# Modulation chunks of a mixer stage dealt over the second part of its steps only

## What is computed

```
mods = (silu(c) @ ada_w + ada_b).reshape(B, 3, 3, 1, D_MODEL)
def modulate(t, i):
    return t * (1.0 + mods[:, i, 1]) + mods[:, i, 0]
def residual(t, i, out, w):
    return _layer_norm(ALPHA * t + w * (1.0 + mods[:, i, 2]) * out, ln_g[i], ln_b[i])
x = residual(x, 0, _swiglu(modulate(x, 0), ...), 0.5)
o_rw, o_gla, o_ml = rwkv7(proj), gla(proj), mlstm(proj)      # proj = modulate(x, 1) @ w_in
x = residual(x, 1, concatenate([o_rw, o_gla, o_ml]) @ w_out, 1.0)
x = residual(x, 2, _swiglu(modulate(x, 2), ...), 0.5)
```

## Time and profile before

| What | us |
|---|---|
| Median of the runs | 1889.33 |
| The profiled execution | 1889.8 |
| Its span in the trace | 1888.0 |
| TensorE busy with matmuls | 1742.9 |
| VectorE busy | 977.2 |
| ScalarE busy | 678.6 |

### The profile page before, as it was taken

One profiled execution on the slowest core, in us unless ns is written; L12 is line 12 of the kernel. 1 busy time (PEld: TensorE's weight loads), 2 busy tenths in 40 slices (PEclk: granted clock), 3 DMA queues, 4 the chain that ended last, 5 costly groups with the idle time before them and its releaser, 6 DMA issues.

```text
span 1888.0 us, 33548 instructions
## 1 busy us (share of the span) xinstructions
PE 1742.9 (92%) x14420; PEld 1568.9 (83%) x14420; DVE 977.2 (52%) x1623; ACT 678.6 (36%) x949; POOL 170.6 (9%) x217
## 2 busy tenths in 40 slices
PE   5999998988899788999989999989989996899997
PEld 2899997987768477999979999979867765799997
DVE  2444445585633476555454444458574336655544
ACT  2333334463211435333353333355532123543333
POOL 1000011002001021000110000110020011300011
PEclk9999998999855598999999999999988557899998
DMA  8556545423232145444456555463323112344442
GB/s 325 182 199 212 190 150 188 162 95 118 92 118 68 48 151 189 146 149 153 147 176 211 180 184 174 153 209 108 115 70 129 57 48 79 117 157 146 156 145 73
DMA packets 85203, 272.36 MB, mean 144 GB/s; under 512 B 18976, under 2 KB 21312, under 8 KB 84800
## 3 DMA queue, kind: packets, MB, share of 16 engines
q1 hardware_dynamic: 80640, 267.60, 41.7%
q10 hardware_dynamic: 4416, 2.62, 0.5%
HBM read 263.92 MB, written 6.26 MB: 143 GB/s over the span
## 4 chain that ended last, share of the span: by engine, by line
PE 78%; DVE 11%; DMA 4%; ACT 4%; issue 2%; SPq 0%; POOL 0%; DVEq 0%; ACTq 0%; POOLq 0%
PE psV L1824 11%; PE psV L1826 11%; PE psV L1825 11%; PE psA L1824 9%; PE psA L1825 9%; PE psA L1826 9%; DMA raw<-weights_dram 4%; PE psC L1839 3%; DVE wlo L2098 3%; PE psV L671 2%; ACT whi L1980 1%; PE psY L1839 1%; DVE PJ L1357 1%; PE psV L1849 1%; PE psV L1442 1%
## 5 line engine op out<-in xcount | busy, mean ns | idle before, releaser
L2098 DVE TENSOR_TENSOR wlo<-raw,whi 128x1024 fp32r<-128x1024 f32 x344 | 425.1, 1239 | 459.7 <-ACT whi L1980 457.9
L1980 ACT ACTIVATE whi<-raw 128x1024 fp32r<-128x1024 f32 x344 | 362.2, 1055 | 343.8 <-PE psV L1826 338.7
L1824 PE MATMUL psA<-XH,whi 128*128 128x320 f32 x1200 | 381.6, 318 | 20.3 <-DVE XL L2150 11.5
L1825 PE MATMUL psA<-XL,whi 128*128 128x320 f32 x1200 | 375.9, 313 | 0.0
L1826 PE MATMUL psA<-XH,wlo 128*128 128x320 f32 x1200 | 375.5, 313 | 0.0
L1824 PE MATMUL psV<-XH,whi 128*128 128x320 f32 x848 | 269.9, 318 | 13.2 <-DVE wlo L2098 7.2
L1825 PE MATMUL psV<-XL,whi 128*128 128x320 f32 x848 | 266.0, 314 | 0.0
L1826 PE MATMUL psV<-XH,wlo 128*128 128x320 f32 x848 | 265.7, 313 | 0.0
L1824 PEld LDWEIGHTS psA<-XH,whi 128*128 128x128 f32 x1200 | 230.4, 192 | 35.1 <-issue 27.9
L1825 PEld LDWEIGHTS psA<-XL,whi 128*128 128x128 f32 x1200 | 230.2, 192 | 0.3
L1826 PEld LDWEIGHTS psA<-XH,wlo 128*128 128x128 f32 x1200 | 230.0, 192 | 0.0
(11 more groups left out here) (368 smaller groups left out, 1914.1 us busy)
## 6 DMA issues: line engine op xcount, KB each, us to landing
raw<-weights_dram SPq DMA_DIRECT2D x488, 512.0 KB, 3.3
ZS<-st_rw_dram SPq DMA_DIRECT2D x2, 768.0 KB, 4.7
S<-st_gla_dram ACTq DMA_DIRECT2D x2, 768.0 KB, 5.1
o_glas_dram<-S SPq DMA_DIRECT2D x2, 768.0 KB
o_rws_dram<-ZS SPq DMA_DIRECT2D x2, 768.0 KB
CON<-consts_dram SPq DMA_DIRECT2D x1, 1288.5 KB, 9.5
XT<-xT_dram SPq DMA_DIRECT2D x1, 1280.0 KB, 9.8
yT_dram<-XT SPq DMA_DIRECT2D x8, 160.0 KB
```

The costliest lines, as they stand in the source:

```text
L1824: mm(out, whi[:, n % SPL, k], hi[:, kt], start=first, stop=False)
L1825: mm(out, whi[:, n % SPL, k], lo[:, kt], start=False, stop=False)
L1980: activation(whi[:, n % SPL], raw[:, DENSE[n] % RAW], ACT.Copy).then_inc(hi_done, 1)
L2098: tt(wlo[:, n % SPL], raw[:, DENSE[n] % RAW], whi[:, n % SPL].bitcast(F32), ALU.subtract).then_inc(lo_done, 1)
```

## The change

The items of `in_tail` are no longer spread over all 57 steps. `together` is put out bare, and all 40 (or 30) items are spread over the 31 later steps. Nothing else differs: the same chunks in the same order, so `LOADS` is the same list too, and the same mixer steps in the same order.

```
     together = spread([(rw[0], int(k > 1)) for k in range(RW_INVERSE)], first)
     heads, ends = GL_STEPS - GL_FIRST, ML_STEPS - ML_FIRST
     other = (ml + gl) * 6 + su + (ml + gl) * (heads - 6) + su + ml * (ends - heads)
-    together += spread([(rw[0], 1)] * (RW_CHUNKS + RW_SAMPLES - 1), other)
-    out += spread([(step, 1) for step in together], ada_groups(in_tail) if in_tail else [])
+    late = spread([(rw[0], 1)] * (RW_CHUNKS + RW_SAMPLES - 1), other)
+    out += together + spread([(step, 1) for step in late], ada_groups(in_tail))
```

## The result

| What | before | changed |
|---|---|---|
| Median, us (4 runs each, same chip) | 1881.57 (1871.8 to 1890.78) | 1909.4 (1906.18 to 1911.61) |
| Ratio with 95% interval | | 1.0132 [1.0079, 1.0184] |
| Span of the profiled execution, us | 1888.0 | 1906.2 |

The four in the table are two of each group, so that their median, 1881.57, lies where hardly a run is. Eight runs of the changed kernel, e8's among them, lie between 1906.2 and 1921.4, with a median of 1911.2. Set against the large sample the change costs 19 us, 1.0%, and the two traces differ by 18.2 us; the one of before is from the larger group. I go by the traces from here. Each is one execution.

The account below looks back on a forecast made before the run. It took TensorE at the half clock to bound the later steps. Gains of 8.1 and 3.7 against costs of 15.8, 10.3 and 1.0 gave +15.3; with -4.6 from the clock, 1889.8 became 1900.5 us, range 1880 to 1918.

Parts of the forecast that it names:

- the second rival: Steps up to the inverse: without chunks as fillers TensorE idles longer and its clock falls earlier, 1916.5 us; chance 0.23.
- both clock cases: TensorE's clock rising in the later steps (1870 us) or falling in the steps up to the inverse (1916.5 us).
- A1, gain 8.1: First layer, steps up to the inverse: 6.1 us of TensorE's work comes back, and 1.9 us from ScalarE.
- The part that wasn't a matmul: First layer, up to the inverse: without ScalarE's group copy, `gl`'s exponentials start earlier and VectorE's wait goes, gain 1.9 us.
- B1, cost 15.8 + 1.0: First layer, later steps: 13 more chunks and 3 more folds cost 15.8 us, new waits for copies 1.0 us.
- The two new waits: First layer, later steps: at two places a group's first chunk must wait for ScalarE's copy, some 0.5 us each.
- These two I let cancel: Second layer's lost full clock from 1432 to 1446, 5.7 us, set against as much gained in the first layer.
- the 10.3 of the sum: Second layer, later steps: added chunks 10.1 us and folds 0.9 and about 0.3, less 1.0 falling into a wait.
- A2, gain 3.7: Second layer, steps up to the inverse: six chunks and half a microsecond ahead of L718 come back, 3.7 us together.
- L767 in the second layer, -4.6: Near the end of the second layer's steps the clock rises as in the first, shortening L767 and L772, twice 2.3 us.
- The clock rising in B: Later steps: added chunks lift TensorE's clock; 1870 us if a third of the work runs at full clock; chance 0.15.
- The cost hidden: Later steps: slack that the busy figure hides takes up the moved chunks, time about 1890 us; chance 0.05.

Follow-up runs that it names:

- e8: The changed kernel run once more, nothing altered, beside other follow-up runs and the kernel before: 1913.88 us, ratio 1.0118.
- e4: The changed kernel plus 24 idle matmuls, results never read, ahead of L700 in each layer: 1895.14 us, ratio 1.0006.
- e1: The kernel before with the change made in the first layer only: 1901.17 us, ratio 1.0066.
- e9: The changed kernel with only 64 of 256 columns computed in each chunk's matmuls in the mixer steps: 1890.37 us, ratio 1.0008.
- e6: The kernel before, order unchanged, plus 24 idle matmuls ahead of L700 in each layer: 1879.64 us, ratio 0.9916.
- e7: Against the kernel before, all items over the 26 steps up to the inverse, plus 24 idle matmuls ahead of L700: 1877.74 us, ratio 0.9932.
- e2: The kernel before with the change made in the second layer only: 1906.57 us, ratio 1.0076.
- e5: The changed kernel with six of each chunk's eight matmuls left out in the mixer steps: 1911.78 us, ratio 1.0103.
- e10: Against the kernel before, items over the steps up to the inverse and the first eight later ones, plus 24 idle matmuls: 1880.7 us, ratio 0.9974.
- e3: Against the kernel before, the move turned round: all items over the 26 steps up to the inverse, later steps bare: 1879.95 us, ratio 0.9938.
- e11: Against the kernel before: first layer same order plus idle matmuls ahead of L700, second layer all items up to the inverse: 1871.09 us, ratio 0.9933.

## Why the prediction came out as it did

The result, 1909.4 us, lies inside the range of 1880 to 1918 and between the forecast (1900.5) and the second rival (1916.5). The range was made to hold most of both clock cases, so that lying in it says little for the mechanism; by the prediction's own line (up to 1908.2 can't be told from no change, chance 0.60) the time is "slower", to which it gave 0.29. The traces differ by 18.2 us where the sum had 10.7. They say why: the sums over the first layer's instructions held, the second layer's clock didn't, and A2 gave back 0.9 us less than its list of chunks.

**A1, gain 8.1: held, 8.2** (6.7 up to L700, where the list had 6.2, and 1.5 from there to L718, where it had 1.9). There is no instruction on `psC` in A any more. Windows with only instructions on `psC`, A1 and B1, against the earlier trace rows:

```profile
444.40:514.20 69.80, 0.00 (x0) 0.00 (x0) 0.00 (x0) 0.82 0.01 2
514.20:635.60 121.40, 28.43 (x224) 6.10 (x224) 2.28 (x6) 0.53 0.38 125
```

The part that wasn't a matmul came too. The timeline of the changed kernel has `gl`'s exponentials at 493.6 us (the prediction had 498) and VectorE's copy behind them, against the earlier trace rows:

```profile
493.57 0.74 ACT L1206 ACTIVATE GZ<-GB 128x640 f32<-128x640 f32 x1
...
504.66 0.17 DVE L1255 COPY GPC<-GZ 128x8 f32<-128x8 f32 x1
```

VectorE's row has no bracket now, the wait of 1.91 us is gone. (The prediction's "some 9 and 7 us of TensorE's work taken out" doesn't agree with its own bounds, 12.7 and 8.6; no term of the sum uses it.)

**B1, cost 15.8 + 1.0: held, 16.6.** There are 224 matmuls on `psC`, 28 chunks, in 28.43 us: 1.015 each, against 1.01. TensorE was busy 117.98 of 121.40 us, 97%. The two new waits are exactly the two that the prediction named, by the waits and the timeline of TensorE in B1, and each the 0.5 us that it gave them:

```profile
PE psC L1839 <- ACT MR L2041: 1.0, 2, 0.5
PE psV L1186 <- ACT PJ L1225: 0.7, 1, 0.7
```

```profile
592.94 1.08 PE L1839 MATMUL psC<-raw,CT 128*32 128x256 f32 x8 [0.50 <-ACT MR L2041]
...
620.30 1.08 PE L1839 MATMUL psC<-raw,CT 128*32 128x256 f32 x8 [0.50 <-ACT MR L2041]
```

No wait for a load appears in these answers.

**"These two I let cancel": this step failed.** The second layer's loss of its full clock was priced at 5.7 us and set off against the same gain in the first. The loss came. The gain didn't. TensorE's timeline ahead of L700 in the changed kernel, first layer, and the windows behind it in the second layer, against the earlier trace rows:

```profile
507.87 0.85 PE L700 MATMUL psA<-TK,AM 64*64 64x64 f32 x21 [2.27 <-DVE Tt L1028]
```

```profile
1436.00:1440.00 4.00, 1.72 (x56) 1.56 (x52) 3.82 (x8) 0.00 (x0) 0.00 (x0) 1.00 0.02 4
1440.00:1444.00 4.00, 3.86 (x91) 3.53 (x88) 0.95 (x3) 1.47 (x3) 0.00 (x0) 0.62 0.02 4
1444.00:1448.00 4.00, 3.98 (x71) 3.82 (x69) 0.00 (x0) 1.67 (x4) 0.00 (x0) 0.50 0.00 0
```

In the first layer the idle stretch shrank from 3.04 to 2.27 us, in the second it grew from 1.86 to 2.28. The prediction had one case of a fall (3.04) and one of none (1.86). It never worked out how long the stretch would be, and took the first layer's for harmless because VectorE's wait went away. Both stretches came out between the two cases, the clock fell in both, and the layers now are alike: A2 69.87 and A1 69.79 us, L718 4.07 us in both. B2 cost 5.5 us more than the 10.3 of the sum, and between L700 and L718 A2 took 1.0 us longer though a chunk of 0.5 had gone: 7.0 us, where the prediction had priced 5.7 and set it to nothing. e4 shows that this is the clock's doing.

**A2, gain 3.7: failed, 1.3.** Of the 2.4 us that are missing, 1.5 are those between L700 and L718 above. Up to L700 2.3 us came of the 3.2 in the list. The clock is down for longer there too (over A its mean went from 0.90 to 0.82), but the record doesn't bear that out as the reason: the first layer's mean fell likewise, from 0.88 to 0.82, and its gain came in full, and e1's first layer, with the very same steps, ran up to L700 at 0.87 in 63.8 us, the changed kernel's at 0.84 in 63.4. So the 0.9 us stay unexplained.

**L767 in the second layer, -4.6: held in size, but half of it was lost behind it.** L767 took 2.97 us as forecast, against 5.29, and L772 behind it 3.12 against 5.27, 4.5 us together. The timeline shows L767, with L1186 and its wait ahead of it:

```profile
1554.08 4.58 PE L1186 MATMUL psV<-PJ,CON 96*96 96x320 f32 x8 [0.72 <-ACT PJ L1225]
1561.86 2.97 PE L767 MATMUL psA<-WT,ZS 64*64 64x8 f32 x96
```

The wait fell from 1.73 to 0.72 us, the -1.0 of the sum. But three chunks now stand behind L767 where two stood, which the sum left out, and two folds instead of one. So the next large product (L801) starts only 2.2 us earlier behind L767. The last part, from L801 to the output product, is 1.8 us shorter, and that is a draw. It takes 8.8 to 9.1 us when L806 finds the full clock and 10.5 to 10.8 when it doesn't, in all 26 layers of the table. The two layers of e8, whose second layer has the list of the changed kernel's:

```profile
669.91 1.88 PE L806 MATMUL psV<-N,CON 128*128 128x320 f32 x6 [1.67 <-ACT N L888]
...
1599.51 3.57 PE L806 MATMUL psV<-N,CON 128*128 128x320 f32 x6 [1.67 <-ACT N L888]
```

In the changed kernel's trace it was 1.88 us in the second layer, in the trace before 3.36. That is why the rest of this layer is 38.7 us in one run of the changed kernel and 40.7 in the other, and why only about 2 of its 4.0 us are due to the change.

**The rivals.** The clock rising in B: refuted, 0.53 and 0.51. The cost hidden: refuted, by e9. The clock falling in A: right in its second-layer half and in that A's mean clock fell, to 0.82; the first layer had nothing to lose, since its clock was already down before L718, so half of its price of 11.4 us had nothing to fall on. The prediction's own bound for it ("in A below 0.8") would have missed it at 0.82: the last fall sits in the last 6 us of A and is mostly paid in B.

With the two corrections the sum is 1900.5 + 5.5 + 2.4 = 1908.4 us, against 1907.9 of the profiled execution; what is left (+0.5 in the first layer's rest, -1.3 outside the stages, the 1.8 us of L806's draw against the chunk and fold behind L767, and smaller terms) cancels. That this comes so near is luck in part.

**What stays open.** Why the clock falls in B at all isn't settled: where it was full at L718, it fell 5 to 34 us behind it, with TensorE mostly 97% busy; the falls of e4 at 1460 and of e6's second layer at 1440 have no idle stretch that I could name. Whether a steady filling through B would hold it wasn't tried. Nor was the idle stretch ahead of L700 varied by itself: every run that changed its length also changed how busy TensorE was ahead of it. What parts the runs of the kernel before into two groups is open too, as no trace of the faster group was taken.

## What to carry to other kernels

Work that only fills an engine's waiting time can also be what holds its clock. Before moving it, read the idle stretch that it leaves ahead of the next long dense part, and price the half clock over that whole part, not over the stretch. Where such a stretch can't be filled with useful work, a few idle matmuls of under 3 us can pay back two to five times their length, but only there: in e6's second layer the same ones cost 3.2 us net, in e7's first layer 1.1, and in e7's second nothing. Read single layers, not only the medians: a part whose clock is a draw (here L801 to the output product, 1.8 us) moves a layer as much as a small change does.

## What the runs showed of the hardware

- In ten layers of these kernels with a bare A, one without chunks (the changed kernel twice, e1, e2, e5, e9) TensorE idled 2.27 or 2.28 us before L700, and each time the single matmuls behind it went from 0.22 to 0.31 us; in two of the ten, the first layers of e1 and e9, the clock was back by L718 (2.47 us), in the others not (4.07). After 1.86 us it fell in none of two. Length alone doesn't decide, though: in e10's second layer it held through 2.56 us, and in the second layers of e3 and e11 it fell with 3.46 us but was back by L718 (2.48 us).
- 24 idle matmuls in 2.80 us kept the full clock for 21 us behind them in e4's second layer and for 29 in e6's first, and B there was shorter by 14.8 and 15.5 us.
- TensorE can be 97 to 98% busy for over 100 us with small fp32 matmuls and be granted the half clock for nearly all of it.
- Two matmuls of a chunk take 0.99 us and eight 1.01: the eight stand in four column groups and must overlap, since a quarter of them takes as long as all. With a quarter of the columns in each, the eight took 0.37 us, so here the columns set the price and not the count.
- The kernel before varied by 1.7% from run to run, and its mean granted clock with it: 0.906 to 0.917 in the 21 runs below 1879 us, 0.890 to 0.905 in the 58 above 1887.
